# Sub-keys folded into the query weights during the attention, and scores in three rounded passes

## What is computed

```python
def peer_ffn(h, w_query, sub_keys, expert_u, expert_v):
    q = (xt @ w_query).reshape(t, PEER_HEADS, 2, D_HALF)        # 512 x 1024 @ 1024 x 2048
    scores = jnp.einsum('thpd,hpnd->thpn', q, sub_keys)         # 16 halves of 128 keys of 128
    sv, si = lax.top_k(scores, PEER_TOPK)                       # 16 of 128, for each half
    ...                                                         # 256 sums of pairs, the best 16, softmax
    # for each token: out = sum over the 128 chosen e of gate_e * gelu(expert_u[e] . x) * expert_v[e]
```

## Time and profile before

| | us |
|---|---|
| three runs | 1633.74, 1632.2, 1626.24 |
| median | 1632.2 |
| profiled execution, first to last instruction | 1627.5 |
| TensorE busy in it | 1569.0 (96%) |
| VectorE busy in it | 1229.0 (76%) |
| ScalarE busy in it | 701.6 (43%) |
| mean granted TensorE clock | 0.982 |

### The profile page before, as it was taken

How to read it: one execution, slowest core, us unless ns; L and a number is a source line. 1 busy time by engine, 2 the same in 40 slices (tenths; PEclk the granted TensorE clock), 3 DMA queues, 4 the chain that set the end, 5 groups by cost and what they waited for, 6 DMA issues and landing times.

```text
span 1627.5 us, 23131 instructions
## 1 busy us (share of the span) xinstructions
PE 1569.0 (96%) x7853; PEld 1341.1 (82%) x7853; DVE 1229.0 (76%) x2271; ACT 701.6 (43%) x1286; POOL 400.8 (25%) x326
## 2 busy tenths in 40 slices
PE   6999899999989999999999999999999999999996
PEld 6887755455589999999989999998888888888885
DVE  5778743289459988898888977548888888888888
ACT  3523434112258734686348843333333333333333
POOL 1002400001023300132002344303344444344420
PEclk9799999999999999999999999999999999999998
DMA  8774700001159976699658999969999999999992
GB/s 315 264 269 170 254 36 0 1 1 52 52 185 366 358 286 195 222 357 379 219 167 286 372 383 360 395 248 340 359 338 359 358 348 340 349 358 358 344 326 95
DMA packets 173062, 425.78 MB, mean 262 GB/s; under 512 B 13357, under 2 KB 62509, under 8 KB 169785
## 3 DMA queue, kind: packets, MB, share of 16 engines
q1 hardware_dynamic: 86688, 265.37, 44.0%
q0 software_dynamic: 36864, 134.23, 23.2%
q10 hardware_dynamic: 49432, 25.19, 5.4%
HBM read 372.32 MB, written 52.43 MB: 261 GB/s over the span
## 4 chain that ended last, share of the span: by engine, by line
PE 85%; DVE 6%; DMA 5%; ACT 1%; issue 1%; POOL 1%; ACTq 0%; SPq 0%; DVEq 0%
PE bank L1262 10%; PE bank L1263 10%; PE bank L1266 10%; PE bank L1207 9%; PE bank L1208 9%; PE bank L1209 9%; PE bank L1151 7%; PE bank L1222 5%; PE bank L1134 3%; DMA weights<-in_uT 2%; DMA weights<-in_expert_v 2%; PE bank L1071 1%; PE bank L1072 1%; PE bank L1073 1%; PE bank L1009 1%
## 5 line engine op out<-in xcount | busy, mean ns | idle before, releaser
L1207 PE MATMUL bank<-h_hi,u_hi 128*128 128x384 f32 x1024 | 349.9, 342 | 7.5 <-DVE h_lo L1633 4.3
L1208 PE MATMUL bank<-h_lo,u_hi 128*128 128x384 f32 x1024 | 344.4, 336 | 0.0
L1209 PE MATMUL bank<-h_hi,u_lo 128*128 128x384 f32 x1024 | 344.3, 336 | 0.0
L1262 PE MATMUL bank<-v_hi,w_hi 128*128 128x512 f32 x768 | 299.1, 389 | 1.7 <-DVE w_lo L1741 1.7
L1263 PE MATMUL bank<-v_lo,w_hi 128*128 128x512 f32 x768 | 299.0, 389 | 0.0
L953 ACT ACTIVATE v_hi<-weights 128x1024 fp32r<-128x1024 f32 x128 | 135.9, 1061 | 331.1 <-PE bank L1266 288.2
L1639 DVE TENSOR_TENSOR u_lo<-weights,u_hi 128x1024 fp32r<-128x1024 f32 x128 | 156.5, 1223 | 115.4 <-PE bank L1209 80.3
L1266 PE MATMUL bank<-v_hi,w_lo 128*128 128x512 f32 x768 | 236.6, 389 | 0.0
L1737 DVE TENSOR_TENSOR v_lo<-weights,v_hi 128x1024 fp32r<-128x1024 f32 x128 | 157.7, 1232 | 94.8 <-ACT v_hi L953 94.6
L1207 PEld LDWEIGHTS bank<-h_hi,u_hi 128*128 128x128 f32 x1024 | 194.2, 190 | 10.3 <-DVE u_lo L1639 5.2
L1208 PEld LDWEIGHTS bank<-h_lo,u_hi 128*128 128x128 f32 x1024 | 194.4, 190 | 0.0
(11 more groups left out here) (284 smaller groups left out, 2305.8 us busy)
## 6 DMA issues: line engine op xcount, KB each, us to landing
weights<-in_uT SPq DMA_DIRECT2D x128, 512.0 KB, 5.7
weights<-in_expert_v SPq DMA_DIRECT2D x128, 512.0 KB, 6.2
gates_dense<-weights SPq DMA_DIRECT2D x24, 1024.0 KB, 7.9
weights<-gates_dense ACTq DMA_DIRECT2D x16, 1536.0 KB, 26.9
shared<-gelu_dense SPq DMA_DIRECT2D x64, 384.0 KB, 7.3
shared<-in_w_ada SPq DMA_DIRECT2D x16, 1024.0 KB, 5.3
gelu_dense<-weights SPq DMA_DIRECT2D x32, 384.0 KB, 5.5
gelu_dense<-ada SPq DMA_DIRECT2D x32, 384.0 KB, 4.9
```

The lines of the kernel that those rows point to most:

```text
L1207: nc.tensor.matmul(a, uh[:, k, :], h2_hi[:, :, k, :], start=(k == 0), stop=False)
L1208: nc.tensor.matmul(a, uh[:, k, :], h2_lo[:, :, k, :], start=False, stop=False)
L1209: ins = nc.tensor.matmul(a, ul[:, k, :], h2_hi[:, :, k, :], start=False, stop=(k == KC - 1))
L1262: nc.tensor.matmul(acc, wh, v_hi[:, r % 2, cols], start=begin, stop=False)
```

## The change

Each of the 16 halves p of the query weights is multiplied on the chip with its sub-keys ("fold"): two folds for each half, each of 4 float32 matmuls of 128 columns, one fold in each of the 32 attention iterations. ScalarE rounds the fold to hi and VectorE subtracts for lo; both parts are stored to DRAM for every half, and read back in four groups of four halves. The scores of one tile and one group (a "visit") are then 24 rounded matmuls of 512 columns and one copy. Eight visits (tiles 0 and 1) stand at n = 33 to 38, 44 and 45, eight (tiles 2 and 3) after the loop. Tile 0's transpose moves from n = 25 to 31. The transposed tile is rounded to hi and lo straight from its bank. 19 products stand beside the selection of tile 1, the closing loop is two bodies (14 and 15) with 30 dots in it, and expert_v, stored products and gates are first loaded there. The gelu of tile 0's dots and its multiplication with the gates move behind the first output.

```diff
-BESIDE = {1: (0,) * 19 + (3,), 2: (1,) * 18 + (0, 0), 3: (1,) * 18 + (0, 0)}
+BESIDE = {1: (1,) * 19 + (0,), 2: (1,) * 18 + (0, 0), 3: (1,) * 18 + (0, 0)}
-LOOP_AT = 12
+LOOP_AT = 14
-DOTS_AT_SEGMENTS = (2, 5, 8, 11, 14)
-DOTS_PER_BODY = {12: 12, 13: 12, 14: 10}
+DOTS_AT_SEGMENTS = {1: (8, 11, 14, 17), 2: (2, 5, 8, 11, 14), 3: (2, 5, 8, 11, 14)}
+DOTS_AT_LOOP = (2, 2, 2, 2, 2, 2, 2, 2, 2, 2, 2, 2, 2, 2, 2, 0)
...
-EARLY_SEGMENTS = 10
+TURN_H_AT = {t: after_head(t, TURN_H) if t else len(ATTN) - 1 for t in range(NT)}
+QGROUPS, QPARTS, RAW_Q, STAGED_Q = 4, 4, 3, 2
+FOLDS = 2 * HP
+FOLD_BANK = (1, 2, 3) * 3 + (1, 2, 3) + (0, 2, 3, 0) + (0,) * 3 + (1,) * 8 + (0,) * 5
+VISITS = {len(ATTN) + 1: (0, 0), len(ATTN) + 2: (0, 1), len(ATTN) + 3: (1, 0), len(ATTN) + 4: (1, 1),
+          len(ATTN) + 5: (2, 0), len(ATTN) + 6: (2, 1),
+          after_head(NT - 1, ADD_1): (3, 0), after_head(NT - 1, ADD_1) + 1: (3, 1)}
+LATE_VISITS = [(g, t) for g in (3, 2, 1, 0) for t in (2, 3)]
+WK_LOADS = [(1, None), (2, (0, 1)), (3, (1, 1)), (1, (3, 3)), (0, (2, 3))]
+EARLY_SEGMENTS = 5
...
 # SyncE
+            for p in range(HP):
+                wait_full(sp, "fold", 2 * p + 1)
+                if p + RAW_Q < HP:
+                    load_wq(p + RAW_Q)
+                wait_read(sp, "fold", 2 * p)
+                wait_read(sp, "fold", 2 * p + 1)
+                store_folded(p)
+            for b in range(STAGED_Q):
+                sp.wait_ge(fold_stored[b], 32 * HP // STAGED_Q)
+            for g, last_use in WK_LOADS:
+                if last_use:
+                    was_g, was_t = last_use
+                    wait_full(sp, "score", was_t, was_g)
+                load_wk(g)
...
 # ScalarE, in the attention loop
+            def fold_hi(u):
+                p, s = u // 2, u % 2
+                b = wait_full(act, "fold", u)
+                if p >= QPARTS + STAGED_Q:
+                    act.wait_ge(fold_stored[p % STAGED_Q], 32 * (p // STAGED_Q))
+                nc.scalar.activation(folded(p)[0][:, 4 * s:4 * s + 4, :], b[:, :].rearrange("p (k n) -> p k n", k=4),
+                                     ACT.Copy).then_inc(fold_hi_made, 1)
...
             for r in range(BODY):
-                if r % RAW == 0:
-                    load_g(r // RAW, r // RAW)
+                if r in (0, 2):
+                    load_g(r // 2, r // 2)
                 loop_product(ITERS - 1, r, False)
...
 # TensorE, in the attention loop (fold) and in visits (score)
+            def fold(u):
+                p, s = u // 2, u % 2
+                if s == 0:
+                    pe.wait_ge(wq_in[p % RAW_Q], 32 * (p // RAW_Q + 1))
+                b = start("fold", u)
+                for k in range(4):
+                    at = (4 * s + k) * P
+                    ins = nc.tensor.matmul(b[:, k * P:(k + 1) * P], wq_raw[:, p % RAW_Q, at:at + P], key_raw[:, p % RAW_Q, :],
+                                           start=True, stop=True)
+                done(ins, "fold", u)
...
+                for k in range(KC):
+                    nc.tensor.matmul(rows, hi[:, k, :], wk_hi[b][:, :, k, :], start=(k == 0), stop=False)
+                    nc.tensor.matmul(rows, hi[:, k, :], wk_lo[b][:, :, k, :], start=False, stop=False)
+                    ins = nc.tensor.matmul(rows, lo[:, k, :], wk_hi[b][:, :, k, :], start=False, stop=(k == KC - 1))
...
 # VectorE, in the attention loop
                 if n < len(ATTN):
                     row_max(n)
+                if 1 <= n <= FOLDS:
+                    fold_lo(n - 1)
...
             def step(K, odd, r, first):
                 if first:
+                    if m == 0:
+                        sparse_weights()
                     loop_add(J, r)
```

More of the change, by code:

```diff
@@ L136, in plan_banks @@
     jobs += [(("cum",), 6)]
-    jobs += [(("sgu", b), b) for b in range(4)]
     jobs += [(("S", n), 4 + n % 2) for n in range(len(ATTN))]
     jobs += [(("PT", n), 6 + n % 2) for n in range(len(ATTN))]
[L140 to L145, removed]
-    for n in range(LAST + 1):
[L148 to L157, removed]
+    for n in range(LAST + 1):
+        if 1 <= n <= 4:
+            jobs += [(("sgu", n - 1), n - 1)]
+        if 0 <= n - VALUES_BEHIND < len(ATTN) and ATTN[n - VALUES_BEHIND][1] == 0:
+            jobs += [(("O", ATTN[n - VALUES_BEHIND][0]), ATTN[n - VALUES_BEHIND][0] % 2)]
+        for s, step in enumerate((MIX_0, MIX_1)):
+            jobs += [(("mix", t, s), 2 + s) for t in tiles_at(n, step)]
+        jobs += [(("h2T", t, s), 2 + s) for t in range(NT) if TURN_H_AT[t] == n for s in range(2)]
+        jobs += [(("yT", t, s), 2 + s) for t in tiles_at(n, TURN_Y) for s in range(2)]
+        if n < FOLDS:
+            jobs += [(("fold", n), FOLD_BANK[n])]
+    jobs += [(("score", t, g), 4 + v % 4) for v, (g, t) in enumerate(SCORED)]
     jobs += [(("turn", d), 5) for d in range(DENSE)]
@@ L166, in program @@
 def program(nc, x, cT, w_ada, b_ada, norm1_gT, w_in, b_f, sg_ln_g, sg_ln_b, sg_wT, sg_bT,
-            out_gT, w_out, norm2_g, w_query, sub_keysT, uT, expert_u, expert_v, final_g, out):
+            out_gT, w_out, norm2_g, w_queryT, sub_keysT, uT, expert_u, expert_v, final_g, out):
     place = plan_banks()
@@ L527, in load_a @@
                     .then_inc(a_in[b], 16)
-            with sp.Fori(LOOP_AT, FEW_DOTS_AT) as I:
-                for r in range(BODY):
-                    loop_product(I, r, True)
             wait_full(sp, "turn", DENSE - 1)
@@ L535, in _ @@
             for r in range(BODY):
[L536 removed]
+                loop_product(LOOP_AT, r, True)
                 if r < RAW:
@@ new lines, in score @@
+            def score(g, t, load):
+                b = WK_BUFFER[g]
+                if load:
+                    pe.wait_ge(wk_in[b], 32 * load)
+                else:
+                    wait_read(pe, "fold", 2 * QPARTS - 2)
+                    wait_read(pe, "fold", 2 * QPARTS - 1)
+                for half in range(2):
+                    wait_read(pe, "h2T", t, half)
+                hi, lo = h2_parts(t)
+                out_bank = start("score", t, g)
+                rows = out_bank[:, :].rearrange("p (j n) -> p j n", j=QPARTS)
+                for k in range(KC):
+                    nc.tensor.matmul(rows, hi[:, k, :], wk_hi[b][:, :, k, :], start=(k == 0), stop=False)
+                    nc.tensor.matmul(rows, hi[:, k, :], wk_lo[b][:, :, k, :], start=False, stop=False)
+                    ins = nc.tensor.matmul(rows, lo[:, k, :], wk_hi[b][:, :, k, :], start=False, stop=(k == KC - 1))
+                done(ins, "score", t, g)
```

238 lines of the change are left out of this document (110 added, 128 removed).

## The result

The change makes the kernel slower, by about half a percent. Six runs of the changed kernel have a median of 1639.43 us (1634.36 to 1646.14), six of the kernel before on the same chip 1630.57 (1626.24 to 1634.17); the ratio is 1.0055, with a 95% interval of 1.0035 to 1.0074. The prediction had 1626 us, 6 under the median shown then; it became 9 over. The profiled execution took 1634.36 us, 1632.2 of it span: it is the fastest of the six, 5 us under their median. Against the span of before, 1627.5, it shows 4.7 us of the loss; the rest is dealt with under the experiments.

The account below looks back on a forecast made before the run. TensorE was taken to bound nearly everywhere, with memory full in the closing loop. Product 0 at -12.6, closing loop +4 and outputs +2.5 gave -6 on the 1627.5 us span; carried to the median 1626, range 1608 to 1643.

Parts of the forecast that it names:

- the closing loop: Last products before the outputs: traffic beside 16 products instead of 32 costs +4 us (-2.7 to +17).
- the crowded loop: Rival: memory holds the closing loop, net about +5 us, 1637; chance 0.12.
- the slow clock: Rival, attention: short waits put TensorE on 1.2 GHz for 14 iterations, net +18 us, 1650; chance 0.12.
- after, it can hold it for 6 to 14, and TensorE bears about 6: Closing loop: the second gate load, 2 products after the first, holds ScalarE 6 to 14 us, TensorE about 6.
- The crowd: Closing loop: 32 MB, 83 us of memory at 384 GB/s, against 66 us of TensorE.
- TensorE's own work: Attention and visits: query groups out -136.2 us, folds in +30.9, visits in +87.1, net -18.2.
- same-bank waits: Attention: a fold going to the previous fold's bank waits for VectorE's subtraction; ten times 0.8, 8 us.
- those of the values: Attention, n = 19 and 27: the values wait for the fold's subtraction, 1.4 + 1.6 us.
- +17 of new waits: Attention: waits the folds bring, 8 + 3 + 4 + 2 us (0 to 30).
- The store's stall: Attention, from half 6: ScalarE's rounding of the fold waits for a store to land; taken as 2 us (0 to 10).
- The reload wait: Late visits: groups 1 and 0 of the folded weights arrive late, +3.5 us (0 to 12).
- The start of the products: Before product 0: TensorE waits some 4.8 us for the first split row instead of 4.3, +0.5.

Follow-up runs that it names:

- all edits but the gates': Against all four repairs: both gate loads back at the first and third product of the last body, 2 products apart; 1625.24 us, 0.9961 of before.
- all but the dots': Against all four repairs: the 6 sparse rows go back from the selections into the closing loop; 1625.19 us, 0.9968 of before.
- the loads far apart: Against the changed kernel: second gate load issued 6 products after the first instead of 2; 1635.50 us, 1.0031 of before.
- all four repairs: Changed kernel with earlier first gate load, later v rows and gelu blocks, 6 dots moved into selections, first u rows rounded before the last copy; 1617.00 us, 0.9929.
- the later rows: Against the early gate load: first four v rows and first four gelu blocks read one body later; 1629.78 us, 1.0001 of before.
- the dots instead: Against the early gate load: 6 of the loop's 30 sparse rows moved into the selections of tiles 2 and 3; 1631.03 us, 1.0012 of before.
- the early gate load: Against the changed kernel: first gate load issued 6 products earlier, 8 products ahead of the second; 1632.43 us, 1.0007 of before.
- the fold alone: Against the changed kernel: no products beside selection 2, 32 products and 34 sparse dots in the closing loop; 1665.26 us, 1.0211 of before.

## Why the prediction was wrong

The direction was wrong, and one term did it: *the closing loop*, forecast at +4 (-2.7 to +17), measured at +15.1 in the profiled execution and some 17 in a typical one (193.52 us to the last gelu for 176.59). The range, 1608 to 1643, held the time only because it was stretched past the crowded loop's 1637 toward the slow clock's 1650, and the slow clock never came: that is luck. The prediction's own sign of being wrong, "if the closing loop loses over 10 us", is what happened.

**The step that failed** is "after, it can hold it for 6 to 14, and TensorE bears about 6". The hold came where it was foreseen, at 11.08 us. But TensorE stood 11.59 us behind it, some 10 of them the hold, not 6. (The term of the sum was even smaller, +4; nothing in the prediction says where its 6 went.) In before a hold of 5.02 us cost TensorE nothing that its waits show: from 1025 to 1100 us these are 1.7 in all, for rows of u. ScalarE was ahead there; it had waited 0.72 us for its row of u, and the wait for rows of over 4 us came only later:

```profile
1032.53 1.06 ACT L852 ACTIVATE u_hi<-weights 128x1024 fp32r<-128x1024 f32 x1 [0.72 <-DMA weights<-in_uT]
...
1037.60 0.49 ACT L860 ACTIVATE ada<-bank 128x384 f32<-128x384 f32 x1 [4.01 <-issue]
```

After, ScalarE came to the load with nothing in hand: it had just waited 4.61 us for its row of u. The two losses were set down side by side, a hold with some cover and a crowd with four rows in hand; they share the one cover. The trace shows it: the wait for u up to 1058.06, the issue right behind it, the gelu read 0.05 us after the issue's end. And where the rows of u were in time, with all edits but the gates', TensorE bore 8.3 of 15.84, and with all but the dots' nothing of 6.30. In all TensorE waited 14.8 us in the loop for 1.7 before: 13.1 of the 15.1 us. Most of the rest is the lower clock behind the waits: behind the long one 8 matmuls start 0.32 us apart, not 0.17.

**The crowd** itself was in the sum as 83 us of memory against 66 of TensorE, and "some 4 MB of gathers and the second gate block may land later without harm". That was the second half of the error. With the hold gone, 9.6 us of waits were left, 6.8 for u rows and 2.8 for gelu reads behind them. And what lands later is not without harm: the outputs behind run at a DMA share of 0.97 too (the last row of the first view; before had 0.99 there), so a late gate block or row is paid at their start (w_lo: 7.6 us with the loads far apart, 7.9 with the dots back). From all four repairs, putting any one of the three back costs 8 to 10 us by the medians, 5 to 8 by the ratios to before. One by one, from the changed kernel on, the gate loads brought 7 to 8, the later rows 1 more and the dots instead nothing, both within the noise. So the hold has a price of its own, much the same alone and last; the parts of the crowd pay only once the others are in order. I had made rivals of the hold and the crowd; both are in the 15 us.

**What held.** TensorE's own work: a fold is 0.95 us (176.81 to 177.76) for 0.96, a rounded pass of a visit 0.227, and product 0 came 13.8 us earlier for 12.6. In the order of time, the first fold and two neighbouring passes of a visit:

```profile
176.81 1.11 PE L1180 MATMUL bank<-weights 128*128 128x128 f32 x8
...
177.76 0.39 PE L1130 MATMUL bank<-shared 128*128 128x128 f32 x2
...
395.31 0.39 PE L1200 MATMUL bank<-wk_hi,h_lo 128*128 128x512 f32 x1
395.54 0.39 PE L1198 MATMUL bank<-wk_hi,h_hi 128*128 128x512 f32 x1
```

The Trainium skill's formula ("TensorE: Matmul & The Clock Gate", Back-to-back issue gap) gives 216 ns for a lone matmul of 512 columns at the higher clock; the rows after the change show 227, as those before did.

The same-bank waits are 7.7 us in 11 places, forecast 8 in ten (its own figures, 3.1 less 2.42, give 0.68 each and not 0.75; measured 0.70); those of the values 2.7, forecast 3.0. But they are no price: with half of them gone nothing came earlier, so "+17 of new waits" was a right list, but its terms don't add up as prices, and that product 0 came out within 1.2 us of the sum is in part luck; the attention is paced by its chain through VectorE and ScalarE, and TensorE's waits only say on which name it falls. The store's stall was 3.4 us at TensorE for 2, and clock 0.88 over 202 to 216; taking it away gave 1.9, with 1.2 more of waits for reloads. The reload wait was 2.1 for 3.5. The start of the products waited 4.58 us for the 4.3 of the earlier trace rows, as "+0.5" has it; that it could be had for nothing by an order on ScalarE was not seen.

**Selection 2** lost 2.0 us, not 0: 1.0 for a split row at the end, 0.55 for the gates, the rest not looked into beyond a slow start of product 0. **The outputs** lost 0.5 for +2.5: the one wait for w_lo is 1.8 us, and the clearing of tile 0 is mostly covered.

The rival "the closing loop is held by memory" (1637) was given 0.12, though the earlier trace rows had a share of 1.02 and the earlier trace rows a hold and a late row in before, with twice the products to hide them. It deserved the most. Its time is the nearest of all to the measured one, but by its mechanism alone the early gate load would have brought under 4 us, and it brought 7 to 8. The rivals of the hidden folds, of the slow clock in the attention (0.99 there) and of visits that wait for reloads are out. Two reasons given there misread the rows: VectorE is busy for 51.09 of 103.35 us in the attention, 49% and not 65, and from 231.70 on the waits before were not shorter, up to 2.08 us, at clock 0.96.

Open is how far the memory balance would bear another cut: no kernel here has more than 6 dots moved.

## What to carry to other kernels

When products are moved away from a stretch, what they were hiding stays behind: add up the bytes that must still pass beside what is left, and if the stretch behind it is full as well, "lands later" is not free. Before adding a stall to a sum, ask whether its cover is already spent by another: two waits with one slack cost their sum, not the larger excess. And a wait that goes when its cause is removed proves nothing until the end moves: here the 11.6 us wait went with the loads moved apart, and the end moved by 4. Edits that brought 1 us or nothing when added singly were worth 6 to 10 when left out of the working set: where several things fill one resource, price each by leaving it out.

## What the runs showed of the hardware

The issue of a transfer can hold the engine that issues it while an earlier transfer on the same queue is still on its way. For gate blocks of 1.5 MB, with a second load 8.2 us behind the first the issue took 15.84 us; 12.0 to 12.3 us behind, 11.08 to 12.32 (three kernels); 17.5 and 17.9 us behind, 5.02 and 9.52; 28.6 us behind, 3.41; 47.7 us behind and more, 0.40. In the kernel with 15.84 it ended 24.1 us after the first load's issue, in the changed kernel 23.4, in before 22.6, in the one with the fold alone 27.4.

That is no fixed time, though, and it is not the whole of the first transfer: in the changed kernel the hold ended 5.3 us before the first load landed (28.7 us after its issue). With all four edits an issue 33.2 us behind took 0.40 us, while the first load landed only after 51.4. At this distance the issue took 0.40, 3.75, 6.30 and 7.37 us in four kernels, and the first two of these have the same closing loop; so what decides is not shown.

The Trainium skill ("DMA: Bandwidth & Descriptors", Specifications) has about 358 GB/s as the limit of a core, half of the 716 of its memory stack. This kernel runs on one core, and the trace shows more than that half: 405 and 403 GB/s in two slices of 25 us of the kernel with all four edits, and 414 in one of the changed kernel. What a second core would leave of it no run here shows.

The clock falls with a wait: over the 25 us slice that holds the idle 11.59 us TensorE's granted clock was 0.75, so part of it was spent at the lower of its two levels, 1.2 and 2.4 GHz. The matmuls behind the wait start 0.32 us apart, 8 of them, and then every 0.17:

```profile
1070.28 0.52 PE L1246 MATMUL bank<-h_lo,u_hi 128*128 128x384 f32 x1
1070.60 0.52 PE L1247 MATMUL bank<-h_hi,u_lo 128*128 128x384 f32 x1
```

In the loop with all four edits, without such a wait, it was 0.98 to 1.00.
